# Seven block products for eight: the up projections of the last two feed-forwards of a float32 transformer stack

## The reference, cut to what matters

```python
D_FF = 2816                              # 22 tiles of 128 channels
...
    x = layer_norm(DEEPNORM_ALPHA * x + mix, ln1_g, ln1_b)

    u = depthwise_conv_centred(x @ w_up, conv_w, conv_b)   # w_up: 1024 x 5632, three taps over the tokens
    gate, val = jnp.split(u, 2, axis=-1)
    ffn = (jax.nn.silu(gate) * val) @ w_down               # w_down: 2816 x 1024
    return layer_norm(DEEPNORM_ALPHA * x + ffn, ln2_g, ln2_b)
```

## Time and profile before

| | before |
|---|---|
| median of 3 runs | 3240.03 us (3238.53 to 3240.19) |
| profiled execution, first to last instruction | 3237.6 us |
| TensorE busy | 3182.1 us, 98% |
| VectorE / ScalarE / GpSimdE busy | 1591.0 / 1301.7 / 1329.3 us |
| granted TensorE clock, mean | 0.995 of full |
| bytes read from HBM | 283.47 MB |

### The profile page before, as it was taken

The page is one execution under the profiler, slowest core; times in us unless marked ns, Lnnn a source line. Parts: engine busy times, 40 slices in busy tenths (PEclk is TensorE's granted clock), DMA queues, the critical chain, the costliest instruction groups (busy, mean ns, idle before and its releaser), DMA issues.

```text
span 3237.6 us, 40142 instructions
## 1 busy us (share of the span) xinstructions
PE 3182.1 (98%) x16204; PEld 2552.9 (79%) x16204; DVE 1591.0 (49%) x2605; ACT 1301.7 (40%) x2307; POOL 1329.3 (41%) x754
## 2 busy tenths in 40 slices
PE   7999999999999999999999999999999999999998
PEld 4876888888885557888886888888887788878886
DVE  5877366323337663423225685352432768455252
ACT  4322421312246774423334535342433544444243
POOL 2222423222254445444551234544455234454446
PEclk9999999999999999999999999999999999999999
DMA  7223334121132003233232111323223121222321
GB/s 274 105 96 121 124 110 147 49 66 66 52 115 103 20 8 116 93 93 105 82 117 72 54 59 53 117 93 101 96 90 114 46 70 45 62 98 76 116 79 55
DMA packets 85925, 288.17 MB, mean 89 GB/s; under 512 B 9803, under 2 KB 10379, under 8 KB 84972
## 3 DMA queue, kind: packets, MB, share of 16 engines
q1 hardware_dynamic: 85740, 285.60, 26.0%
HBM read 283.47 MB, written 2.10 MB: 88 GB/s over the span
## 4 chain that ended last, share of the span: by engine, by line
PE 89%; DVE 3%; issue 2%; POOL 2%; ACT 2%; DMA 1%; SPq 0%; POOLq 0%; DVEq 0%; ACTq 0%
PE ps L504 20%; PE ps L507 20%; PE ps L505 20%; PE ps L563 2%; PE ps L565 2%; PE ps L564 2%; PE ps L2153 2%; PE ps L3005 1%; PE ps L2596 1%; DMA ring<-in_w_mod 1%; PE ps L483 1%; PE ps L2223 1%; PE ps L478 1%; PE ps L522 1%; PE ps L2610 1%
## 5 line engine op out<-in xcount | busy, mean ns | idle before, releaser
L452 POOL TENSOR_TENSOR WL<-ring,WH 128x1024 fp32r<-128x1024 f32 (+2 forms) x427 | 926.6, 2173 | 1397.4 <-ACT WH L441 1397.0
L504 PE MATMUL ps<-HX,WH 128*128 128x512 f32 x1656 | 649.2, 392 | 0.0
L507 PE MATMUL ps<-HX,WL 128*128 128x512 f32 x1656 | 647.7, 391 | 0.0
L505 PE MATMUL ps<-HX,WH 128*128 128x512 f32 x1656 | 646.2, 390 | 0.0
L441 ACT CAST WH<-ring 128x1024 fp32r<-128x1024 f32 (+2 forms) x443 | 421.1, 951 | 529.5 <-PE ps L507 471.2
L504 PE MATMUL ps<-FR,WH 128*128 128x512 f32 x1120 | 418.8, 374 | 0.3
L505 PE MATMUL ps<-FR,WH 128*128 128x512 f32 x1120 | 409.7, 373 | 0.0
L507 PE MATMUL ps<-FR,WL 128*128 128x512 f32 x1120 | 389.4, 373 | 0.0
L504 PEld LDWEIGHTS ps<-HX,WH 128*128 128x128 f32 x1656 | 311.1, 188 | 67.2 <-issue 1.2
L507 PEld LDWEIGHTS ps<-HX,WL 128*128 128x128 f32 x1656 | 312.3, 189 | 45.0
L505 PEld LDWEIGHTS ps<-HX,WH 128*128 128x128 f32 x1656 | 311.3, 188 | 45.0
(11 more groups left out here) (406 smaller groups left out, 5271.8 us busy)
## 6 DMA issues: line engine op xcount, KB each, us to landing
ring<-in_ffn_w_up SPq DMA_DIRECT2D x88, 512.0 KB, 3.2
ring<-in_w_up SPq DMA_DIRECT2D x88, 512.0 KB, 3.2
ring<-in_w_mod SPq DMA_DIRECT2D x64, 512.0 KB, 4.2
ring<-in_w_in_tok SPq DMA_DIRECT2D x40, 512.0 KB, 3.3
ring<-in_w_mod_columns SPq DMA_DIRECT2D x32, 512.0 KB, 4.1
ring<-in_w_in_feat SPq DMA_DIRECT2D x32, 512.0 KB, 3.2
ring<-in_ffn_w_down SPq DMA_DIRECT2D x32, 384.0 KB, 3.0
ring<-in_w_out SPq DMA_DIRECT2D x32, 384.0 KB, 3.1
```

Source lines behind the costliest of these rows:

```text
L452: pool.tensor_tensor(WL[:, p % SPLITS, 0:n], ring.ap(r), WH[:, p % SPLITS, 0:n], ALU.subtract).then_inc(*ring.frees(r, split.g, "low", p))
L504: pe.matmul(o, high, xh, first, False)
L505: pe.matmul(o, high, xl, False, False)
L507: m = pe.matmul(PS[bs[i]][:, 0:N], low, get(k)[0], False, last)
```

## The change

The first two pairs of each of the two feed-forwards (FRONT = 2) stay as they are. Each of the other 20 pairs is computed as a 2 x 2 block product by seven block products instead of eight. The blocks are gate and value, the lower and upper half of k (4 tiles each), and the first and last 256 tokens. Sums of weight blocks are made by VectorE from the two raw tiles of a pair (`sums_1_2`, `sums_3_4`), differences of input blocks once per feed-forward (`forms_v`, split by `forms_a` and `forms_g` into four tiles XF). Each product is 12 matmuls of 256 columns, and the results are combined in PSUM, by matmuls that add to what is there, by 256-wide copies on ScalarE and by two 256-wide sums on VectorE. A pair has four units: "11" (one product), "3 12", "1 2" and "4 22" (two each). In iteration i TensorE runs 11 of pair i, 3 12 of pair i-1, 1 2 of pair i, 4 22 of pair i-1. VectorE makes the rest of "1 2", GpSimdE those of the others. Both raw tiles of a pair stay in the ring until the rest of 4 22.

The down groups are cut in panels of 3, 4, 5, 5 and 5 tiles, and stand in fours behind iterations 4, 6, 8, 10, 13, 15 and 18; one stands in iteration 22 and eleven at the end. The ring has 8 slots instead of 9, and FR 10 instead of 12 for these two feed-forwards. Value biases are negated at the start of the program. VectorE's adds into X after a down group are now 40 per feed-forward instead of 16.

```diff
-SLOTS = 9
+SLOTS = 8
...
+FRONT = 2
...
+        def seven_plan(name, wname, dname, i):
...
+            L.sizes, L.nst, L.i, L.slots = [3, 4, 5, 5, 5], 1, i, 10
...
+            def made(kind, j, n, loads=()):
+                p = L.unit[kind, j] = len(ring.splits)
+                ring.splits.append((None, n))
+                ring.made[p] = (L, kind, j)
+                if loads:
+                    ring.carried[p] = [((L.name, x), up[x]) for j_ in loads for x in (2 * j_, 2 * j_ + 1)]
...
+            after = {4: 4, 6: 4, 8: 4, 10: 4, 13: 4, 15: 4, 18: 4}
+            for j in range(FRONT, FT + 1):
+                if j < FT:
+                    made("11", j, 512, range(j, min(j + 2, FT)) if j == FRONT else range(j + 1, min(j + 2, FT)))
+                if j > FRONT:
+                    made("3 12", j - 1, 1024)
+                if j < FT:
+                    made("1 2", j, 1024)
+                else:
+                    some("between", 1)
+                if j > FRONT:
+                    made("4 22", j - 1, 1024)
+                some(j, after.get(j, 0))
+            some("end", len(rows))
...
+        in_vector |= {p for p, (_, kind, _) in ring.made.items() if kind == "1 2"}
...
+            if kind == "11":
+                return ring.ap(gate)[:, 0:512], ring.landed(gate)
+            if kind == "3 12":
+                return ring.ap(gate), sv.v.at("sum 3", L.name, j)
+            if kind == "1 2":
+                return T[:, 4:6, :].rearrange("p a b -> p (a b)"), sv.v.at("sum 2", L.name, j)
+            return ring.ap(val), sv.v.at("sum 4", L.name, j)
...
+            if kind == "4 22":
+                for r in raw_tiles(L, j):
+                    ring.frees_too(r, steps)
...
+        def forms_v(dve, q):
+            for k in range(4):
+                dve.wait_ge(*nm.a.at("kept", q.name, k + 4))
+                b12, b21, b22 = BLOCKS[:, 2 * k + 1, :], BLOCKS[:, 2 * k + 8, :], BLOCKS[:, 2 * k + 9, :]
+                dve.tensor_tensor(raw_form(k, F1, 2).rearrange("p (a b) -> p a b", a=2), BLOCKS[:, 2 * k:2 * k + 10:9, :],
+                                  b12.unsqueeze(1).to_broadcast([128, 2, 256]), ALU.subtract).then_inc(*sv.v.up())
...
+        def forms_a(act, q):
+            for k in range(4):
+                act.wait_ge(*sv.v.at("forms", q.name, k))
...
+        def forms_g(pool, q):
+            for k in range(4):
+                pool.wait_ge(*sv.a.at("forms", q.name, k))
...
+        def product_pe(pe, p, at, out, x, ready=None, opens=None):
+            for k in range(4):
+                c = slice(at + k * 128, at + k * 128 + 128)
+                high, low = WH[:, p % SPLITS, c], WL[:, p % SPLITS, c]
+                xh, xl = x(k)
+                if ready is not None:
+                    for done in ready(k):
+                        pe.wait_ge(*done)
+                if k == 0 and opens == "whole bank":
+                    pe.matmul(out[0], high, HX[:, 0, 0, :], True, False)
+                else:
+                    pe.matmul(out[1], high, xh, k == 0 and opens == "half", False)
+                pe.matmul(out[1], high, xl, False, False)
+                m = pe.matmul(out[1], low, xh, False, k == 3)
+            return m
...
+            for i in range(FRONT, FT + 1):
+                j = i - 1
+                if i < FT:
+                    A[i], B[i] = bank.take_in("gate", "gate", name, i), bank.take_in("val", "val", name, i)
+                    C[i] = bank.take_in("five", "five", name, i)
+                    p = begin("11", i)
+                    if i < FRONT + 2:
+                        pe.wait_ge(*bank.free("val", name, i))
+                        pe.matmul(PS[B[i]][:, :], WH[:, p % SPLITS, 0:128], HX[:, 0, 0, :], True, True)
+                    pe.wait_ge(*bank.free("gate", name, i))
+                    product_pe(pe, p, 0, left(A[i]), block_of(0, 0), None, "whole bank").then_inc(*split.pe.up("used", p))
+                if j >= FRONT:
+                    p = begin("3 12", j)
+                    pe.wait_ge(*sv.a.at("copy 2", name, j))
+                    product_pe(pe, p, 0, right(B[j]), form_of(F3), formed).then_inc(*sv.pe.up("product 7", name, j))
+                    pe.wait_ge(*sv.v.at("five right", name, j))
+                    product_pe(pe, p, 512, left(A[j]), block_of(1, 0)).then_inc(*split.pe.up("used", p))
+                if i < FT:
+                    p = begin("1 2", i)
+                    pe.wait_ge(*bank.free("five", name, i))
+                    product_pe(pe, p, 0, left(C[i]), form_of(F1), formed, "half").then_inc(
+                        *sv.pe.up("product 5", name, i))
+                    pe.wait_ge(*sv.a.at("copy 1", name, i))
+                    product_pe(pe, p, 512, right(B[i]), form_of(F2S), formed).then_inc(*split.pe.up("used", p))
+                else:
+                    for g in L.downs["between"]:
+                        down(g)
+                if j >= FRONT:
+                    p = begin("4 22", j)
+                    product_pe(pe, p, 0, right(A[j]), block_of(1, 1)).then_inc(*sv.pe.up("product 3", name, j))
+                    pe.wait_ge(*sv.v.at("five both", name, j))
+                    product_pe(pe, p, 512, left(B[j]), form_of(F4), formed).then_inc(*split.pe.up("used", p))
+                for g in L.downs.get(i, ()):
+                    down(g)
...
+            forms_a(act, qf)
...
+            for i in range(FRONT, FT + 1):
+                j = i - 1
+                if FRONT < i < FT:
+                    cast_to(act, L.unit["11", i] + 3)
+                high(i - 2)
+                if i == FRONT:
+                    cast_to(act, L.unit["11", i] + 3)
+                if i < FT:
+                    act.wait_ge(*used("11", i))
+                    if i >= FRONT + 2:
+                        act.wait_ge(*bank.free("val", name, i))
+                    act.copy(val_bank(L, i)[:, 256:512], gate_bank(L, i)[:, 0:256]).then_inc(*sv.a.up("copy 1", name, i))
+                if j >= FRONT:
+                    act.wait_ge(*sv.pe.at("product 7", name, j))
+                    act.copy(val_bank(L, j)[:, 0:256], val_bank(L, j)[:, 256:512]).then_inc(*sv.a.up("copy 3", name, j))
+                    cast_to(act, L.unit["3 12", j] + 3)
+                if i < FT:
+                    act.wait_ge(*sv.pe.at("product 5", name, i))
+                    if i >= FRONT + 2:
+                        act.wait_ge(*sv.v.at("five both", name, i - 2))
+                    act.copy(five(i), ps("five", name, i)[:, 0:256]).then_inc(
+                        *bank.emptied(("five", name, i), sv.a, "copy 5", name, i))
+                    act.wait_ge(*used("1 2", i))
+                    act.copy(gate_bank(L, i)[:, 256:512], val_bank(L, i)[:, 256:512]).then_inc(
+                        *sv.a.up("copy 2", name, i))
+                    cast_to(act, L.unit["1 2", i] + 3)
...
+                if j >= FRONT:
+                    act.wait_ge(*sv.pe.at("product 3", name, j))
+                    act.wait_ge(*fw.v.at("low", name, j - 2, 0))
+                    conv_a(act, fw.a, (name, 2 * j, 0), T[:, j % 2, :], gate_bank(L, j)[:, :], cw(1, j), cb(j))
+                    cast_to(act, L.unit["4 22", j] + 3)
+                    act.wait_ge(*used("4 22", j))
+                    act.wait_ge(*sv.v.at("five both", name, j))
+                    conv_a(act, fw.a, (name, 2 * j + 1, 0), T[:, 2 + j % 2, :], val_bank(L, j)[:, :], cw(1, FT + j),
+                           cb(FT + j))
+                    act.wait_ge(*fw.v.at("conv", name, 2 * j, 0))
+                    act.activation(gate_bank(L, j)[:, :], T[:, j % 2, :], ACT.Silu).then_inc(
+                        *fw.a.up("silu", name, j, 0))
+                for g in L.downs.get(i, ()):
+                    down(g)
...
+            def sums_1_2(j):
+                gate, val = raw_tiles(L, j)
+                dve.wait_ge(*ring.landed(val))
+                dve.tensor_tensor(T[:, 4, :], ring.ap(val)[:, 0:512], ring.ap(val)[:, 512:1024], ALU.add).then_inc(
...
+            def sums_3_4(j):
+                gate, val = raw_tiles(L, j)
+                dve.wait_ge(*low_done(L.unit["11", j]))
+                dve.tensor_tensor(ring.ap(gate)[:, 0:512], ring.ap(gate)[:, 0:512], ring.ap(val)[:, 0:512],
+                                  ALU.add).then_inc(*sv.v.up("sum 3", name, j))
...
+            for i in range(FRONT, FT + 1):
+                j = i - 1
+                if i < FT:
+                    rest_v(dve, L.unit["1 2", i])
+                low(i - 2)
+                if j >= FRONT:
+                    dve.wait_ge(*sv.a.at("copy 3", name, j))
+                    dve.wait_ge(*sv.a.at("copy 5", name, j))
+                    dve.tensor_tensor(val_bank(L, j)[:, 256:512], val_bank(L, j)[:, 256:512], five(j), ALU.add).then_inc(
+                        *sv.v.up("five both", name, j))
+                if i < FT:
+                    sums_3_4(i)
+                if i + 1 < FT:
```

(24 more changed lines are left out.)

210 lines of the change are left out of this document (190 added, 20 removed).

## The result

| | before | after |
|---|---|---|
| median, with the lowest and highest run | 3239.65 us (3238.53 to 3240.19) | 3441.4 us (3438.94 to 3445.23) |
| ratio to before, 95% interval | | 1.0621 (1.0606 to 1.0636) |
| profiled execution, first to last instruction | 3237.6 us | 3437.2 us |
| granted TensorE clock, mean | 0.995 | 0.973 |

What follows compares the result with a forecast made beforehand. The prediction took TensorE's gapless matmuls to bound the kernel. Its terms, -37.6 + 93 + 22.5 + 16.4 + 3 + 7.4 + 3 = +107.7, gave 3348 us, with a range of 3275 to 3395.

Steps and rivals of the forecast that it cites:

- the loop through the ring: Feed-forward pairs: release of raw tiles, load, sums and VectorE's rest make TensorE wait; +93 us (51 to 115).
- second iterations: Iterations 6, 8, 10, 12, 15, 17, 20 of each feed-forward, second behind down products: TensorE waits 5.4 us each (3.1 to 6.5).
- third ones: Iterations 13, 18, 21 of each feed-forward, third pair in a row: TensorE waits 2.9 us more (1.3 to 4).
- (b): Feed-forward loop: VectorE works in queue order, so its rest of "1 2" comes late; TensorE waits 3.1 us without collisions.
- (c): Feed-forward loop: VectorE operations with two SBUF inputs stand still beside GpSimdE's subtractions, raising the wait from 3.1 to 5.4 us.
- (e): First iterations, iteration 4 and the last of each feed-forward: waits of 8.2 us, twice +16.4 (10 to 24).
- Term (d): Start of each feed-forward: forms delay the fourth up tile, stalls of 8 and 14.5 us, together +22.5.
- Term (f): Down products: late VectorE and two banks +3 (0 to 6); last eight groups waiting for GpSimdE +7.4 (2 to 14).
- The third rival: TensorE's waits: the clock falls in them, sixteen waits of 5 us or more cost 27 more, 3375 us; chance 0.19.
- the sentence against it: On the clock falling in the waits: dense matmuls stand before and behind these waits.
- term (g): Every other stage: one ring slot less, a lead of one tile less where loads already bind; +3 us (0 to 10).
- the gain of the products: Seven-product pairs: 84 matmuls at 0.117 us save 0.94 us per pair, -37.6 us over forty pairs (-28 to -48).

Runs made afterwards that it cites:

- the floor: Changed kernel with nine slots, earlier start, downs in twos, and sums and rests of the pairs' units over 64 columns: 3250.25 us, ratio 1.0029 to before.

## Why the prediction was wrong

**Right.** What bounds the kernel, and that the loop through the ring would turn TensorE's gain into waits. The waits stand where they were put: in the first feed-forward eight of 4.1 to 4.3 us (one early, then the seven second iterations) and the three third ones 2.4 each. Terms (b), (c) and (e) were 93 + 16.4 = 109; the three rows of the loop sum to 108.

The sum is in part right by luck. The single second-iteration wait was 4.3, between the low end of 3.1 and the 5.4 chosen, and two errors nearly cancel in it. Counted from the start of unit "11" at 2225.62, as the forecast counts, the loads were issued at 5.3 (forecast 5.15) and landed at 10.0 (10.3); the two sums took 4.1 us instead of 2.05, since both met a rest of GpSimdE and the second met one of 2.55 in full; VectorE's rest took 2.9 (2.8) and ended at 20.9 instead of 19.6. TensorE, though, came to wait only at 16.7 instead of 14.3: its matmuls are slower than 0.117, and it had itself waited for GpSimdE's rests, 0.96 us of it before one unit. Such waits are 20 us in 26 places, which no step had named. Iteration 4 waited 4.1 and 4.0 us where (e) had 2.1.

Term (d) was 22.5 and is 22.3, both waits to 0.2 us. The rule of the Trainium skill on the shared pair (SBUF — State Buffer, "SBUF: two separate sides") holds for the block sums and VectorE's rests too: the rows above show them. Term (f) was too high: 10.4 forecast, and 2.4 us in the waits view (`PE ps L1040 <- POOL T L874: 2.4, 1, 2.4`), one wait behind the last down group of the first feed-forward for GpSimdE's sum for the layer norm. The kernel before doesn't have it, and it is one of the 2 us that the term puts there in each; the gaps between these groups are 0.3 us and less.

**Wrong, in order of size.** First, the clock (+47). The third rival had it, with 27 us and as an alternative to the forecast; it was no alternative, since it comes with every wait of the size forecast. The step that failed is the sentence against it: dense matmuls before and behind a wait do not protect it. The row it had was the earlier trace rows, 0.76 for 7 us, and its 1.7 us of loss per wait is 1.95 in the mean here: 31 of the 47 us are lost behind the 16 waits of 4.0 to 4.3 us, 8 behind five of the six of 2.4, 3 behind the two of the start, and the rest behind shorter ones and one of 2.65. The Trainium skill's "HAM oscillation" (TensorE: Matmul & The Clock Gate) said that waits for transfers throttle the clock each time; by that rule 3375 was the case to expect. The trace agrees for all 16 waits of 4.0 us and more and for five of the six of 2.4; these are waits for VectorE's rest, which itself hangs on a load.

Second, term (g), one slot less: +3 (0 to 10) where the trace has +27 and the experiment by itself +29. It was sized by nothing. The profile of before showed six waits for `in_w_mod`, 19.6 us, and the stages with these waits are the ones that lost with eight. Inside the feed-forwards too the loop lacked the slot: it was worth 53 us there and outside together.

Third, the gain of the products: 0.117 us per matmul was chosen between 0.114 and 0.120, and it is 0.120; -28, the low end, instead of -37.6. The purer row of 0.114 was of another form of operands; the new ones are those of the earlier trace rows.

These three are 47 + 24 + 10 = 81 of the 93 us between 3348 and 3441. The rest is the 24 us of seams, for which the forecast had no term, less the 8 that (f) had too much and small differences.

## What to carry to other kernels

Before an edit trades matmul columns for elementwise work and buffers, follow one period of the new loop through every engine and the loads; if its slowest chain is longer than TensorE's work, cures one at a time only move the wait (nine cures, from -9 to -131, none to zero). Add to each wait of some us what the clock takes behind it, as part of the same case. Take a buffer away only after running the old kernel without it, and first run the floor, the kernel with the added work cut short: here one version gives 3250, as slow as before, and shows that in this order no cure of the loop could pay.

## What the runs showed of the hardware

- Behind a wait of 4.29 us between dense matmuls TensorE ran 4.7 us at a granted clock of 0.50. The loss behind waits of this length was 1.1 to 2.5 us in 16 cases, and behind waits of 2.4 us it was 1.5 us in five of six cases and nothing in the sixth, so the length alone doesn't decide. In the floor kernel the clock was low from 2108.6 to 2118.8 us: it fell in a wait of 3.21 us and lasted through one of 1.46 us behind it (starts 0.21 to 0.22 us apart).

```profile
2109.31 0.79 PE L3442 MATMUL ps<-HX,WH 128*128 128x512 f32 x1 [3.21 <-POOL WL L533]
2114.34 0.58 PE L3398 MATMUL ps<-XF,WH 128*128 128x256 f32 x1 [1.46 <-DVE WL L511]
2114.72 0.41 PE L3399 MATMUL ps<-XF,WH 128*128 128x256 f32 x1
2114.94 0.41 PE L3400 MATMUL ps<-XF,WL 128*128 128x256 f32 x1
```

- PE's busy time counts slow matmuls in full (4.69 of 4.70 us at half clock): 3230.5 us against 3182.1 before, with fewer columns computed. The mean clock (0.973) tells what the busy share doesn't.
- VectorE, with two inputs in SBUF, stood still for a subtraction of GpSimdE that had begun before it: its 0.69 us became 2.67, its 1.22 became 2.91. Of the 40 second sums of the changed kernel 18 began beside such a subtraction; all took 2.67 to 2.75 us and ended 0.55 behind it, and the 17 with none beside them took 0.69. The rests ended 1.08 behind it in most cases. A VectorE sum that had begun before GpSimdE's instruction kept its 0.69.
